# Expert routing in two sorted lists with ranks by matrix products, and a start without a meeting ahead of the RWKV pairs

## The reference

```python
x = x + mix
h = rms_norm(x, norm_ffn_g[i])
aff = jax.nn.softmax((h @ w_router).astype(jnp.float32), axis=-1)
gates, idx = lax.top_k(jnp.swapaxes(aff, 1, 2), cap)      # cap = 64 of 512 tokens
xe = h[b_idx, idx]
hid = (jax.nn.silu(jnp.einsum('becd,edf->becf', xe, w_gate))
       * jnp.einsum('becd,edf->becf', xe, w_up))
ye = jnp.einsum('becf,efd->becd', hid, w_down) * gates[..., None].astype(h.dtype)
x = x + jnp.zeros_like(h).at[b_idx, idx].add(ye)
```

## Time and profile before

| | us |
|---|---|
| median of 3 runs | 1900.36 |
| lowest, highest | 1900.03, 1903.24 |
| the profiled execution, whole | 1901.98 |
| its span | 1900.2 |
| TensorE busy | 1772.0 (93%) |
| VectorE busy | 819.0 (43%) |
| ScalarE busy | 559.6 (29%) |
| GpSimd busy | 153.1 (8%) |

### The profile page before, as it was taken

The page is one execution under the profiler, slowest core; times in us unless marked ns, Lnnn a source line. Parts: engine busy times, 40 slices in busy tenths (PEclk is TensorE's granted clock), DMA queues, the critical chain, the costliest instruction groups (busy, mean ns, idle before and its releaser), DMA issues.

```text
span 1900.2 us, 40296 instructions
## 1 busy us (share of the span) xinstructions
PE 1772.0 (93%) x17576; PEld 898.3 (47%) x17576; DVE 819.0 (43%) x1562; ACT 559.6 (29%) x1161; POOL 153.1 (8%) x230
## 2 busy tenths in 40 slices
PE   7999999999999599999988998999996999999998
PEld 4456666666555333333333355666543333333333
DVE  7867777776653412222211234777414222112212
ACT  3456555655542111111110123555320111101110
POOL 2101110111011100000000011111120000000000
PEclk9999999999999799999999998999997999999999
DMA  4101101110314999999999942000276999999998
GB/s 130 37 19 45 38 24 35 45 38 24 110 69 150 366 377 427 428 427 427 427 428 426 417 165 112 24 24 25 98 304 249 428 427 428 427 427 428 427 428 343
DMA packets 92184, 459.69 MB, mean 242 GB/s; under 512 B 16997, under 2 KB 50154, under 8 KB 68202
## 3 DMA queue, kind: packets, MB, share of 16 engines
q1 hardware_dynamic: 89994, 449.78, 58.5%
q0 software_dynamic: 2016, 7.34, 1.0%
HBM read 449.23 MB, written 7.86 MB: 241 GB/s over the span
## 4 chain that ended last, share of the span: by engine, by line
PE 73%; DMA 10%; issue 7%; DVE 3%; ACT 2%; SPq 2%; DVEq 1%; POOL 1%; POOLq 1%; another core or an unknown queue 1%; ACTq 0%; PEldq 0%
PE banks L1780 26%; PE banks L549 9%; DMA arena<-in_moe_w_down 7%; PE banks L1802 5%; PE banks L854 4%; PE banks L1433 4%; DMA arena<-in_moe_w_up 3%; PE banks L2355 3%; PE banks L2220 2%; PE banks L2380 1%; PE banks L2368 1%; PE banks L834 1%; PE banks L566 1%; SPq L1957 1%; PE banks L1748 1%
## 5 line engine op out<-in xcount | busy, mean ns | idle before, releaser
L1780 PE MATMUL banks<-arena 128*64 128x512 f32 x2944 | 657.4, 601 | 32.1 <-DMA arena<-in_moe_w_down 20.2
L1780 PEld LDWEIGHTS banks<-arena 128*64 128x64 f32 x2944 | 209.7, 138 | 442.7 <-issue 411.3
L1945 DVE TENSOR_TENSOR arena<-arena,banks 128x512 f32<-128x512 f32 x128 | 88.1, 688 | 285.1 <-PE banks L1802 285.1
L549 PE MATMUL banks<-arena 128*128 128x512 f32 x384 | 192.1, 618 | 0.0
L1885 ACT ACTIVATE arena<-banks 128x512 f32<-128x512 f32 x32 | 34.1, 1066 | 394.1 <-PE banks L1780 394.1
L1929 DVE SCALAR_TENSOR_TENSOR arena<-arena,banks 128x512 f32<-128x512 f32 x32 | 34.1, 1064 | 217.7 <-ACT arena L1885 217.7
L1802 PE MATMUL banks<-arena 128*128 128x512 f32 x256 | 114.7, 598 | 1.5 <-DVE arena L1942 1.5
L854 PEld LDWEIGHTS banks<-arena 64*64 64x64 f32 x5120 | 83.7, 134 | 62.9 <-issue 51.4
L1932 DVE SCALAR_TENSOR_TENSOR arena<-arena,small,banks 128x512 f32<-128x512 f32 x32 | 35.6, 1112 | 174.6 <-PE banks L1780 174.6
L854 PE MATMUL banks<-arena 64*64 64x64 f32 x5120 | 95.0, 221 | 2.6 <-issue 0.9
L549 PEld LDWEIGHTS banks<-arena 128*128 128x128 f32 x384 | 64.8, 189 | 51.5 <-issue 43.1
(11 more groups left out here) (307 smaller groups left out, 2217.7 us busy)
## 6 DMA issues: line engine op xcount, KB each, us to landing
arena<-in_moe_w_gate SPq DMA_DIRECT2D x64, 2048.0 KB, 32.5
...
```

What stands on the lines that cost most here:

```text
L549: last = nc.tensor.matmul(b[:, :], w_sl[:, n, k, :], xmix[n][:, k, :], start=(k == 0), stop=(k == ND - 1))
L1780: last = nc.tensor.matmul(b[z * CAP:(z + 1) * CAP, :], st[:, k, :], ring[g % RING][:, k, z * 512:(z + 1) * 512], start=(c % 2 == 0 and k = ...
L1945: nc.vector.tensor_tensor(xs, xs, b[:, :], ALU.add).then_inc(free[xj[("add", i, j)][0]], 1)
```

## The change

**Start.** `masks_dve` stands at VectorE's beginning; the levels and the copies of the triangles (`triangles_dve`) are spread between the four normed tiles. A first count of `consts_ready` is given as soon as the two index tables stand. The first low-rank products wait for four transfers of `ld_lora` only; those of the gate count on `ld_gate`.

**No meeting ahead of the pairs.** The five calls of the meeting are gone, and the counts of semaphores and banks run on (`rj` starts from `pj.count`, `nth` adds one for pair jobs). TensorE begins pair 0 with LR of direction 0 as soon as the first operands are ready, does the last gate product (`gate_quarters_pe`) and the turns of v there, and then waits for the second operands. VectorE's gate operations (`gates_dve`) stand between the masks of MR. SP's loads for pair 1 each wait for the product that used the slice.

**Routing.** The affinities of tiles 0 to 2 (384 tokens) are turned and searched while tile 3 is still being multiplied (`early_round`, 64 values in eight rounds, of which three are done beside the late list); those of tile 3 (128 tokens) make a second list. The largest 64 of both lists are the element-wise maximum of one list and the other reversed; its minimum is the limit. A token is chosen when it is above the limit, or equal to it in order of tokens. Ranks come from products with a triangle of ones (`upto`) and ones (`every`): four for each layer, eight in all. The softmax is one ScalarE instruction for each tile, with the largest value as bias and the inverse root as scale. Tile 3 of x is turned by halves, the first while its second half is multiplied. ScalarE's square of tile 3, GpSimd's operations on it and the store order move with it.

**Experts.** `rows_pe` and `combination_pe` of the first pair stand behind the first gate product.

```diff
+            masks_dve(dve)
+            level_dve(dve, 0)
+            level_dve(dve, 1)
+            normed(0)
+            triangles_dve(dve)
+            level_dve(dve, 2)
+            normed(1)
+            level_dve(dve, 3)
+            normed(2)
             turned(0)
-            masks_dve(dve)
+            normed(3)
             turned(1)
             b = job_full(dve, pj, "cols")
             nc.vector.tensor_copy(cols, b[:, 0:V_N * ND]).then_inc(free[pj["cols"][0]], 1)
             dve.drain()
             prep_cols(dve, 0)
             turned(2)
-            levels_dve(dve)
+            level_dve(dve, 4)
...
-            dve.wait_ge(gate_ready, 2)
-            nc.vector.tensor_scalar(gate_a, gate_a, 0.5, 0.5, ALU.mult, ALU.add)
-            nc.vector.tensor_scalar(gate_b[0:GATE - P, :], gate_b[0:GATE - P, :], 0.5, 0.5, ALU.mult, ALU.add)
+
+        def gates_dve(dve):
+            for name, v in (("ga", gate_a), ("gb", gate_b[0:GATE - P, :])):
+                job_read(dve, pj, name)
+                nc.vector.tensor_scalar(v, v, 0.5, 0.5, ALU.mult, ALU.add).then_inc(gate_ready, 1)
...
-                if u:
-                    pe.wait_ge(operands_ready, 2 * u)
+                plain = lambda v: (lambda m: v[:, m * P:(m + 1) * P])
+
+                def values_turned():
+                    job_read(pe, *((rj, ("v", u - 1)) if u else (pj, ("v", 0))))
+                    turn(pe, ("vt", u), plain(vT))
+                    turn_by_heads(pe, 0, u)
+
+                pe.wait_ge(operands_ready, 2 * u + 1)
                 across(pe, "LR", Bt[0], 0, u)
+                if not u:
+                    gate_quarters_pe(pe)
+                    values_turned()
+                pe.wait_ge(operands_ready, 2 * u + 2)
...
-                out(3, 0)
+                out(3, 0, range(3))
                 logits(1)
                 turn_x(2)
-                out(3, 1)
-                logits(2)
             else:
                 out(0, 0, range(NPAIR - 1, ND))
                 out(0, 1)
                 pe.wait_ge(router_ready, 1)
-                for t in range(1, NT):
+                for t in range(1, NT - 1):
                     out(t, 0)
                     turn_x(t - 1)
                     out(t, 1)
                     logits(t - 1)
-            turn_x(NT - 1)
+                out(3, 0, range(3))
+                turn_x(2)
+            out(3, 0, range(3, 5))
+            logits(2)
+            out(3, 0, range(5, 7))
+            select("sel_early", range(NT - 1))
+            out(3, 0, range(7, ND))
+            out(3, 1, range(2))
+            pe.wait_ge(aff_ready, 1)
+            by_expert("at_early", range(NT - 1))
+            out(3, 1, range(2, 4))
+            job_read(pe, oj, ("out", 3, 0))
+            turn_half(3, 0)
+            out(3, 1, range(4, ND))
+            logits_half(3, 0)
+            pe.wait_ge(x_ready, NT)
+            turn_half(3, 1)
+            logits_half(3, 1)
+            select("sel_late", (3,))
+            pe.wait_ge(aff_ready, 2)
+            by_expert("at_late", (3,))
+
+            def to_rows(name, i):
+                b = open_job(pe, oj, name)
+                pe.wait_ge(limit_ready, i + 1)
+                nc.tensor.transpose(b[:, 0:NE], wide_limit[0:NE, i, :], ident[0:NE, 0:NE]).then_inc(full[oj[name][0]], 1)
+
+            to_rows("limit", 0)
+            b = open_job(pe, oj, "rank")
+            pe.wait_ge(above_ready, 1)
+            rank = b[:, 0:2 * NT * NE].rearrange("p (i t e) -> p i t e", i=2, t=NT)
+            nc.tensor.matmul(b[:, 0:2 * NT * NE], upto, above.rearrange("p i t e -> p (i t e)"), start=True, stop=False, skip_group_check=True)
             for t in range(NT - 1):
-                select(t)
-            logits(NT - 1)
-            select(NT - 1)
-            pe.wait_ge(aff_ready, 1)
-            b = open_job(pe, oj, "at")
-            for t in range(NT):
-                last = nc.tensor.transpose(b[0:NE, tile(t)], aff[:, t, 0:NE], ident[:, :])
-            last.then_inc(full[oj["at"][0]], 1)
-            pe.wait_ge(slot_ready, 1)
-            b = open_job(pe, oj, "st")
-            for t in range(NT):
-                last = nc.tensor.transpose(b[:, t * NE:(t + 1) * NE], cumT[0:NE, tile(t)], ident[0:NE, 0:NE])
-            last.then_inc(full[oj["st"][0]], 1)
+                last = nc.tensor.matmul(rank[:, :, t + 1:NT, :], every, above[:, :, t:t + 1, :].to_broadcast([P, 2, NT - 1 - t, NE]),
+                                        start=False, stop=(t == NT - 2), skip_group_check=True)
+            last.then_inc(full[oj["rank"][0]], 1)
+            to_rows("count", 1)
...
+            exponentials("sel_early", range(NT - 1), 1)
+            scaled(2)
+            turned(3)
+            square(3)
+            logits(3)
+            exponentials("sel_late", (3,), 2)
+            scaled(3)
...
+            largest(0, NT - 1, "sel_early")
+            shares(0, NT - 1, "sel_early")
+            added(3, 0)
+            listed("at_early", early_work)
+            for r in range(4):
+                early_round(r)
+            added(3, 1)
+            turned(3)
+            early_round(4)
+            largest(3, NT, "sel_late")
+            dve.sem_inc(hT_read[n], 1)
+            shares(3, NT, "sel_late")
...
+            listed("at_late", late_work)
+            for r in range(CAP // 8):
+                nc.vector.max(late_top[0:NE, 8 * r:8 * r + 8], late_work[0:NE, :])
+                if r < 3:
+                    nc.vector.max(early_top[0:NE, 8 * r + 40:8 * r + 48], early_work[0:NE, :])
+                dve.drain()
+                if r < CAP // 8 - 1:
+                    nc.vector.match_replace(late_work[0:NE, :], late_top[0:NE, 8 * r:8 * r + 8], late_work[0:NE, :], -1.0)
+                if r < 2:
+                    nc.vector.match_replace(early_work[0:NE, :], early_top[0:NE, 8 * r + 40:8 * r + 48], early_work[0:NE, :], -1.0)
+                dve.drain()
...
+            merged = late_work[0:NE, 0:CAP]
+            nc.vector.tensor_tensor(merged, early_top[0:NE, :], late_top[0:NE, ::-1], ALU.max)
+            dve.drain()
+            nc.vector.tensor_reduce(limit[0:NE, 0:1], merged, AX, ALU.min)
+            dve.drain()
+            nc.vector.tensor_copy(wide_limit[0:NE, 0, :], limit[0:NE, 0:1].to_broadcast([NE, P])).then_inc(limit_ready, 1)
+            nc.vector.tensor_scalar(early_work[0:NE, 0:CAP], merged, limit[0:NE, 0:1], None, ALU.is_gt)
             dve.wait_ge(iota_ready, 1)
             nc.vector.tensor_copy(iota_s, iota_i)
+            dve.drain()
+            b = job_full(dve, oj, "limit")
+            per_expert = lambda v: v[:, 0:NE].unsqueeze(1).to_broadcast([P, NT, NE])
+            nc.vector.tensor_tensor(above[:, 0, :, :], aff[:, :, 0:NE], per_expert(b), ALU.is_gt)
+            nc.vector.tensor_tensor(above[:, 1, :, :], aff[:, :, 0:NE], per_expert(b), ALU.is_equal).then_inc(above_ready, 1)
+            nc.vector.tensor_reduce(limit[0:NE, 1:2], early_work[0:NE, 0:CAP], AX, ALU.add)
+            dve.drain().then_inc(free[oj["limit"][0]], 1)
+            nc.vector.tensor_copy(wide_limit[0:NE, 1, :], limit[0:NE, 1:2].to_broadcast([NE, P])).then_inc(limit_ready, 1)
             nc.vector.tensor_copy(row_cols[:, :, :, 0], token_i.unsqueeze(2).to_broadcast([P, NT, NE // 2]))
             nc.vector.tensor_copy(row_cols[:, :, :, 1:3], aff[:, :, 0:NE].rearrange("p t (i c) -> p t i c", c=2))
-            b = job_full(dve, oj, "st")
-            nc.vector.tensor_copy(slot[:, :, 0:NE], b[:, 0:NT * NE].rearrange("p (t e) -> p t e", t=NT)).then_inc(free[oj["st"][0]], 1)
+            ranks = job_full(dve, oj, "rank")[:, 0:2 * NT * NE].rearrange("p (i t e) -> p i t e", i=2, t=NT)
+            b = job_full(dve, oj, "count")
+            nc.vector.tensor_tensor(logit, above[:, 1, :, :], per_expert(b), ALU.mult).then_inc(free[oj["count"][0]], 1)
+            dve.drain()
+            nc.vector.tensor_tensor(above, above, ranks, ALU.mult).then_inc(free[oj["rank"][0]], 1)
+            dve.drain()
+            nc.vector.tensor_tensor(slot[:, :, 0:NE], above[:, 0, :, :], above[:, 1, :, :], ALU.add)
+            dve.drain()
+            nc.vector.tensor_tensor(slot[:, :, 0:NE], slot[:, :, 0:NE], logit, ALU.add)
...
                             if h:
                                 gather_half_pe(pe, 1, xj)
-                            else:
-                                rows_pe(pe, 0, layer)
-                                combination_pe(pe, 0, xj)
                             job_read(pe, xj, ("x", 0, h))
...
                 up_to_hidden(("gate", i, 0), 0, 0)
+                if i == 0:
+                    rows_pe(pe, 0, layer)
+                    combination_pe(pe, 0, xj)
                 up_to_hidden(("up", i, 0), 0, 2)
...
             meet_pool(pool, [])
             start_pool(pool)
-            meet_pool(pool, start_sems + prep_sems, everyone)
             pairs_pool(pool)
...
-            meet(sp, "sp")
```

(6 more changed lines are left out.)

284 lines of the change are left out of this document (152 added, 132 removed).

## The result

The changed kernel takes 1887.45 us, median of four runs (1886.23 to 1890.65), against 1900.31 us of the kernel before; the ratio is 0.993, 95% interval 0.9914 to 0.9945. The forecast was 1883.5, its range 1879 to 1893. The profiled execution has a span of 1885.9 us in a run of 1887.69 us, 14.3 less than the span before.

A forecast was written before the change was run, and what follows sets the result against it. It took the expert weight stream as the bound once refills run, with work ahead counting in full. Start and handover 7.5, layer 0 4.8 and layer 1 4.5 made 16.8 us off, 1883.5 us; range 1879 to 1893.

The forecast's parts named there:

- (a): Expert stages: the weight stream hides routing, so only the start's 7.5 us count, giving 1892.9 us; chance 0.12.
- (d): Routing: narrow VectorE operations cost as much as 512-wide ones, giving 1913 us, chance 0.03; search alone 1898, chance 0.02.
- (b): Start and early search rounds: GpSimd and VectorE hold one another up at the ports, giving 1887 us; chance 0.12.
- (c): Handover to pairs: waiting for second operands replaces the meeting, clock falls, that gain is only 2, 1886.8 us; chance 0.10.
- Part 1: Masks at the start: first mixed operation 3.3 us earlier, less 1.1 for port contention, net 2.2 us.
- the ports: First microseconds: VectorE and GpSimd masks contend for the shared SBUF port pair, costing 1.1 us.
- Part 2: Handover to the pairs without the meeting: the inverse starts 5.3 us earlier, ends 4.0 and 6.5.
- no cover to spare: Ahead of the first inverse: VectorE's work ends near 87.6 us, against the inverse's forecast start at 87.4.
- The pairs: Pair stages: taken as unchanged, with no gain or loss of their own in the sum.
- Part 3: Routing, last output product to first gather: 3.8 us less in layer 0 and 3.5 in layer 1.
- Part 4: First expert chunks: moved rows and combination release chunk 12 1.5 us earlier; worth 1.0 us in each layer.

The follow-up runs named there:

- the second trace of the changed kernel: The changed kernel run once more with nothing altered, for its own spread: 1885.49 us, ratio 0.9923 to the kernel before, span 1882.3 us.

## Why the prediction was right, and where its terms were not

The time fell in the range, 4.0 us above the forecast. The frame held: two stages in which the stream is the bound, and everything ahead of their first refills counts in full. Rivals (a) and (d) are out. Rival (b) gives a number near the time, 1887, for a reason that is not there: beside GpSimd's operation of 1.28 us at 620.16 the early MAX8 took 0.55 us, as without it. So does (c): the LR products of both directions ran at full clock. That the time came out this near is in part luck, since the terms missed by up to 2.5 us either way.

*Part 1.* Gross 3.3 less 1.1 for the ports was forecast. Measured 3.68 at the first mixed operation, and 0.08 for the ports. The Trainium skill ("SBUF — State Buffer", "Who interferes with whom") has the shared port pair as a lock for the whole instruction. The trace does not speak against it: the operation at 4.38 ended at 4.68, GpSimd's, begun before it, at 4.63. What failed is the step from the lock to its price. With operations of 0.2 to 0.4 us on both sides a wait is short: three of VectorE's mask operations took 0.30 to 0.34 us where their like took 0.19 to 0.23 in the trace of before, one 0.29 for 0.23, most others the same, and the list as a whole ended in time for the first norm. What the sum lacked is that TensorE's gap ahead of the first low-rank product stays, 2.1 us as before, and that the clock can fall behind it, a step later; it did in five of eight traces. With the fall 2.3 us reach gb4 (72.78 - 70.51), without it 3.9 (72.78 - 68.86). The sum's 2.2 was right by errors that cancel: 1.0 too much for the ports, 0.4 too little gross, and a fall of 1.4 that it did not have.

*Part 2.* 5.3 forecast, 4.8 measured. The inverse's start won 8.0 of the timeline, 2.3 of it from part 1; the 0.9 lost at its second half was the VectorE bound that the working named ("no cover to spare") and did not price. The meeting itself is 2.9 of the 4.8.

*The pairs.* "Unchanged" is right for the code within about 1 us, by thirteen traces, and 2.5 us wrong for this pair of them. TensorE has a pause of 2.5 to 3.1 us near 500 us in every one of them; in the trace of before the clock was at 1.2 GHz behind it (0.53 in the last row of its stretches above), so 64 products took 3.57 us and not 1.98, in that of the changed kernel not. The other 0.9 lie in steps of 0.1 to 0.5 with no cause that I can name; the new waits on single operands may hold part of it, which was not tried apart.

*Part 3.* 3.8 and 3.5 forecast, 3.4 and 3.1 measured. By its own steps: the products' end moved back 2.2 us, not 3.2; the way to the search took 6.0 (6.2); the search 8.6 (8.1, though its rounds add up to 8.2; of the difference 0.4 is one gap of VectorE that waits for nothing the profile shows); search to gather 6.0 (4.9). The interpolated widths were good to 0.02 us. Two terms are off by about 1 us and cancel: the work put ahead of the products' end, 1.0 too dear, and the last, 1.1 too cheap. There rank products and turns stand on a TensorE that has been idle for 9.9 us, at 1.2 GHz, and VectorE waits 1.72 us for them.

*Part 4.* The step that failed. It was to give 1.0 us a layer and gives about 0.35, and the sum assumed that the gather stays as it was. Chunk 12's end was put at issue + 4.9; a restarted stream needs about 1.6 more, in both kernels alike. That alone would have made the term larger, the full 1.5 us of chunk 12. But the later release of chunk 13 then falls 0.5 us ahead of chunk 12's end and not 3.1, its own start lies open, and that takes back 1.1.

The rest of the -1.14 in layer 0 is the clock, and much of it is chance. The first half of that gather took 1.3 us more than before, at a granted clock of 0.57 instead of 0.73. With the same instructions it took 5.43 in the second trace of the changed kernel, 0.3 more than before, and there the stretch behind it is 429.15, so -0.18 stands in place of -1.14; in layer 1 it is 456.61, +0.59. That the gather is colder because of the shorter search is not shown.

*Attention.* No term, -0.79. In all thirteen traces this stretch is 275.4 to 276.8; the kernel before had the shortest. Nothing of the change is in it.

Of the 14.3 us between the two traces 13.5 are start, handover and routing (2.27 + 4.82 + 3.38 + 3.07), -1.0 is the experts' and 1.7 (2.51 - 0.79) belongs to nothing in the change; the second trace of the changed kernel, 3.6 us shorter than the first with the same instructions, shows how much of such a ledger hangs on where the clock falls and when it comes back.
